# Left-token products of the second weight pair issued ahead of the right half's transposes, and operand sums moved from GpSimd to VectorE

## What is computed

```python
# first block: mixer, then
x = x + gt_m * rms_norm(y_mix @ w_out, g_post_mix)                # "down" 0, e = 0
h = rms_norm(x, g_pre_ffn) * (1 + sc_f) + sh_f                    # boundary 1
gate, val = split(dwconv3(h @ w_up))                              # "up" conv
x = x + gt_f * rms_norm((gelu(gate) * val) @ w_down, g_post_ffn)  # "down" far, e = 1
# second block
# boundary 2
x = layernorm(ALPHA * x + 0.5 * (silu(x @ w1) * (x @ w3)) @ w2)   # "up" 1
x = layernorm(ALPHA * x + mixer(x))                               # "down" mix2, e = 3
# boundary 3
x = layernorm(ALPHA * x + 0.5 * (silu(x @ w1) * (x @ w3)) @ w2)   # "up" 2
```

## Time and profile before

| | us |
|---|---|
| median of three runs (lowest, highest) | 3124.21 (3119.46, 3126.83) |
| span of the profiled execution | 3115.5 |
| PE busy | 2934.1 (94%) |
| DVE busy | 2196.2 (70%) |
| ACT busy | 1251.5 (40%) |
| POOL busy | 282.6 (9%) |

### The profile page before, as it was taken

One profiled execution on the slowest core, in us unless ns is written; L12 is line 12 of the kernel. 1 busy time (PEld: TensorE's weight loads), 2 busy tenths in 40 slices (PEclk: granted clock), 3 DMA queues, 4 the chain that ended last, 5 costly groups with the idle time before them and its releaser, 6 DMA issues.

```text
span 3115.5 us, 36782 instructions
## 1 busy us (share of the span) xinstructions
PE 2934.1 (94%) x13273; PEld 2307.7 (74%) x13273; DVE 2196.2 (70%) x3919; ACT 1251.5 (40%) x2186; POOL 282.6 (9%) x287
## 2 busy tenths in 40 slices
PE   7998889799999999999999998997999799999997
PEld 4875667578888888788888875774547678888886
DVE  7888516989988567766665675999525866665668
ACT  3123435544444554433334443245543333333443
POOL 2141200200000002000000001214420200000000
PEclk9988989899999999999999999998999999999999
DMA  6531023244445773444448632110004344444854
GB/s 226 169 125 21 9 98 119 71 156 156 162 158 195 272 253 109 147 158 159 156 152 316 217 129 66 41 44 16 1 0 152 106 151 156 156 156 167 316 200 148
DMA packets 345410, 436.79 MB, mean 140 GB/s; under 512 B 29685, under 2 KB 191517, under 8 KB 345054
## 3 DMA queue, kind: packets, MB, share of 16 engines
q1 hardware_dynamic: 342274, 428.46, 41.4%
q10 hardware_dynamic: 2956, 5.99, 0.5%
HBM read 317.59 MB, written 116.50 MB: 139 GB/s over the span
## 4 chain that ended last, share of the span: by engine, by line
PE 81%; DVE 12%; ACT 3%; issue 2%; DMA 2%; POOL 1%; SPq 0%; DVEq 0%; ACTq 0%; POOLq 0%
PE psum L1902 35%; PE psum L1359 20%; PE psum L2714 5%; PE psum L1017 5%; PE psum L1893 3%; PE psum L3914 3%; DVE count_junk L3135 2%; PE psum L2904 2%; PE psum L2883 1%; PE psum L414 1%; DMA ada_w<-in_w_ada 1%; PE psum L384 1%; PE psum L3822 1%; DVE x_t L1600 1%; PE psum L2894 1%
## 5 line engine op out<-in xcount | busy, mean ns | idle before, releaser
L1359 PE MATMUL psum<-far_op,far_op 128*128 128x512 f32 x2772 | 629.6, 389 | 0.0
L1359 PEld LDWEIGHTS psum<-far_op,far_op 128*128 128x128 f32 x2772 | 520.0, 188 | 108.2 <-issue 0.3
L1902 PE MATMUL psum<-x_b,w_near 128*128 128x512 f32 x1440 | 347.6, 390 | 3.9 <-DVE w_near L1531 3.9
L1902 PE MATMUL psum<-x_t,w_near 128*128 128x512 f32 x1440 | 337.0, 389 | 0.7 <-ACT psum L1640 0.6
L1902 PE MATMUL psum<-x_t,w_far 128*128 128x512 f32 x1440 | 336.3, 389 | 0.0
L1902 PEld LDWEIGHTS psum<-x_b,w_near 128*128 128x128 f32 x1440 | 271.3, 188 | 60.9 <-issue 4.3
L1902 PEld LDWEIGHTS psum<-x_t,w_near 128*128 128x128 f32 x1440 | 270.0, 188 | 58.0 <-ACT psum L1640 2.0
L1902 PEld LDWEIGHTS psum<-x_t,w_far 128*128 128x128 f32 x1440 | 270.2, 188 | 56.5 <-ACT u_keep L1652 0.4
L1130 DVE TENSOR_TENSOR far_op<-far_a,far_op 128x512 fp32r<-128x512 f32 x231 | 160.7, 695 | 176.2 <-ACT far_op L1123 174.8
L1123 ACT CAST far_op<-far_a 128x512 fp32r<-128x512 f32 x231 | 143.9, 623 | 316.0 <-PE psum L1359 307.9
L1902 PE MATMUL psum<-x_b,w_far 128*128 128x512 f32 x720 | 178.0, 397 | 8.8 <-DVE val_row L1772 8.8
(11 more groups left out here) (499 smaller groups left out, 4967.6 us busy)
## 6 DMA issues: line engine op xcount, KB each, us to landing
far_a<-row_ops SPq DMA_DIRECT2D x231, 256.0 KB, 2.8
row_ops<-hidden SPq DMA_DIRECT2D x99, 512.0 KB, 5.6
raw<-in_ffn_w SPq DMA_DIRECT2D x88, 512.0 KB, 4.5
col_sums<-hidden SPq DMA_DIRECT2D x66, 512.0 KB, 5.7
far_b<-col_sums SPq DMA_DIRECT2D x132, 256.0 KB, 3.2
raw<-in_w_up SPq DMA_DIRECT2D x44, 512.0 KB, 3.8
hidden<-in_ffn_w SPq DMA_DIRECT2D x44, 512.0 KB, 5.1
far_b<-in_ffn_w SPq DMA_DIRECT2D x66, 256.0 KB, 3.2
```

Of the source, the lines that this page charges most:

```text
L1359: ins = t.matmul(bank(b + n), l[slot][:, rows], r[slot][:], start=(fresh and i == 0 and m == 0), stop=(i == FH - 1 and m == 2), skip_group ...
L1902: ins = t.matmul(bank(b), at[:, l, cols], x[:, k, r], start=(start and k == 0 and m == 0), stop=(k == 3 and m == 2), skip_group_check=not ...
```

## The change

At boundaries 1 and 3 (`begun_ahead`) TensorE multiplies, after the left half of pair 0 and before it waits for the right rows, the left half of pair 1: all eight columns of weight 0 and the first four of weight 1 (`ahead`), into banks 4 and 6. The right half's transposes then have banks 5 and 7 only, and two columns are transposed first instead of four. The casts and rests of both of pair 1's first operands are moved ahead of the norm chain of the right rows. `up_tensor` leaves out what was done ahead. The junk tile of the squares moves to another place, since the operand of weight 1 now lies there during the squares.

At all three boundaries `t_pools` goes: VectorE makes the sums b11 ahead of the right columns' rests, b21 in between the first four, and t1 behind the last.

```diff
-    sq_junk = place("sq_junk", [P, 2, HALF], RR + 40 * KB)
+    sq_junk = place("sq_junk", [P, 2, HALF], GR + 84 * KB)
...
-    def t_pools(pool, st):
...
+    def first_sum(dve, st, j):
+        if j == 0:
+            dve.wait_ge(x_lo_made, st.turned(0, 3))
+        nc.vector.tensor_tensor(b11_sum[j][:], x_op["b11"][:, j, 0], x_op["b11"][:, j, 1], ALU.add).then_inc(t_raw, 1)
+
+    def late_sum(dve, st, j):
+        if j == 0:
+            dve.wait_ge(x_lo_made, st.turned(0, KD - 1))
+        nc.vector.tensor_tensor(b21_sum[j][:], x_op["b21"][:, j, 0], x_op["b21"][:, j, 1], ALU.add).then_inc(t_raw, 1)
+
+    def left_differences(dve, st):
         for j in range(4):
+            dve.wait_ge(t_raw, st.first_summed(j))
+            dve.wait_ge(x_kept, st.kept_x(j))
+            nc.vector.tensor_tensor(t_part("t1", j, 1), t_part("t3", j, 0), b11_sum[j][:], ALU.subtract).then_inc(t_raw, 1)
...
     def up_scalar(act, st):
-        cast_op(act, st, 1, 1)
+        if not begun_ahead(st):
+            cast_op(act, st, 1, 1)
         t_upper(act, st, 0)
...
     def up_vector(dve, st):
-        rest_op(dve, st, 1, 1)
+        if not begun_ahead(st):
+            rest_op(dve, st, 1, 1)
+        left_differences(dve, st)
         for wave in range(3):
             t_waves(dve, st, wave)
...
     def up_tensor(pe, st):
                 for half in range(2):
-                    ins = classic_step(1, u, k, half, k == 0, k == KD - 1)
+                    if half or not (begun_ahead(st) and ahead(u, k)):
+                        ins = classic_step(1, u, k, half, k == 0, k == KD - 1)
...
     def end_scalar(act, st, up):
         upper_first(act, up)
+        for i in range(2):
+            cast_op(act, up, 1, i)
         take_root(act, cols_of(1))
...
-        cast_op(act, up, 1, 0)
         upper_second(act, up)
...
     def end_vector(dve, v, steps, st, up):
         lower_first(dve, v, up)
+        for i in range(2):
+            rest_op(dve, up, 1, i)
         if e == 0:
...
+    def begun_ahead(st):
+        return st.e in (0, 3)
+
+    def turn_bank(up, half, k):
+        if half and begun_ahead(up):
+            return bank(5 + 2 * (k % 2))
         return bank(4 + k % 4)
+
+    def ahead(u, k):
+        return u == 0 or k < 4
...
     def lower_second(dve, v, up):
+        for j in range(4):
+            first_sum(dve, up, j)
         for k in range(KD):
...
             v.tensor_tensor(lower, src, upper, ALU.subtract).then_inc(x_lo_made, 1)
-            if k == 3:
+            if k < 4:
+                late_sum(dve, up, k)
+            if k == 3 and not begun_ahead(up):
                 rest_op(dve, up, 1, 0)
...
     def end_tensor_up(pe, st, up):
         def turn(half, k):
-            if half and k < 4:
-                pe.wait_ge(x_lo_made, up.turned(0, k + 4))
+            if half and k < 2:
+                pe.wait_ge(x_lo_made, up.turned(0, KD - 1))
             elif half:
-                pe.wait_ge(x_kept, up.kept_x(k - 4))
+                pe.wait_ge(x_kept, up.kept_x(k - 2))
...
-            for k in range(4):
+            lead = 2 if half else 4
+            for k in range(lead):
                 turn(half, k)
...
-                if k + 4 < KD:
-                    turn(half, k + 4)
+                if k + lead < KD:
+                    turn(half, k + lead)
+            if half == 0:
+                for u in range(2):
+                    pe.wait_ge(op_lo, up.op(1, u))
+                    for k in range(KD):
+                        if ahead(u, k):
+                            classic_step(1, u, k, 0, k == 0, k == KD - 1)
...
     def blocks_gpsimd(pool, steps):
-        t_pools(pool, up_conv)
-        t_pools(pool, up_1)
         mix2_gpsimd(pool, steps)
-        t_pools(pool, up_2)
```

More of the change, by code:

```diff
@@ L780, in body @@
     rows_mm, ROWS_0 = glu_mm, 6
-    t_pool, T_POOL_0 = win_lo, len(win_units)
+    t_raw, T_RAW_0 = win_lo, len(win_units)
     before = {"units": 0, "evac": 0, "ups": 0, "act": 0}
@@ L915, in summed, with first_summed, late_summed, t1_made @@
             return T_SUM_0 + 12 * self.q + 4 * wave + j + 1
-        def pooled(self, i):
-            return T_POOL_0 + 12 * self.q + i + 1
+        def first_summed(self, j):
+            return T_RAW_0 + 12 * self.q + j + 1
+        def late_summed(self, j):
+            return T_RAW_0 + 12 * self.q + 4 + j + 1
+        def t1_made(self, j):
+            return T_RAW_0 + 12 * self.q + 8 + j + 1
         def t_made(self, o, j):
@@ L1547, in t_part @@
         return x_f32[name][:, j, part]
-    def t_pools(pool, st):
-        g = nc.gpsimd
-        pool.wait_ge(x_lo_made, st.turned(0, KD - 1))
-        pool.wait_ge(x_hi_made, st.turned(1, 0))
-        for j in range(4):
[L1555 to L1561, removed]
+    def first_sum(dve, st, j):
[7 more added lines that the diff above has]
+    def left_differences(dve, st):
+        for j in range(4):
+            dve.wait_ge(t_raw, st.first_summed(j))
+            dve.wait_ge(x_kept, st.kept_x(j))
+            nc.vector.tensor_tensor(t_part("t1", j, 1), t_part("t3", j, 0), b11_sum[j][:], ALU.subtract).then_inc(t_raw, 1)
     def t_waves(dve, st, wave):
@@ L1570, in t_waves @@
                 dve.wait_ge(x_kept, st.kept_x(4 + j))
-                dve.wait_ge(t_pool, st.pooled(4 + j))
+                dve.wait_ge(t_raw, st.t1_made(j))
                 ins = v.tensor_tensor(t2, b22, t1, ALU.subtract)
@@ L1576, in t_waves @@
                 dve.wait_ge(t_sum, st.summed(0, j))
-                dve.wait_ge(t_pool, st.pooled(8 + j))
+                dve.wait_ge(t_raw, st.late_summed(j))
                 ins = v.tensor_tensor(t4, b21_sum[j][:], t2, ALU.subtract)
@@ L1587, in t_upper @@
             if o == 2:
-                act.wait_ge(t_pool, st.pooled(4 + j))
+                act.wait_ge(t_raw, st.t1_made(j))
             else:
@@ L2246, in far_end_ln @@
         split_columns(dve, v, 1)
-    def turn_bank(k):
+    def begun_ahead(st):
[3 more added lines that the diff above has]
+            return bank(5 + 2 * (k % 2))
         return bank(4 + k % 4)
+    def ahead(u, k):
+        return u == 0 or k < 4
     def kept_column(k):
@@ L2265, in upper_first @@
                 act.wait_ge(xt_turned, up.turned(0, k))
-                s.copy(upper, turn_bank(k)).then_inc(x_hi_made, 1)
+                s.copy(upper, turn_bank(up, 0, k)).then_inc(x_hi_made, 1)
             if e == 0 and k % 2:
@@ L2277, in rest @@
             dve.wait_ge(x_hi_made, up.turned(0, k))
-            src = split_tmp[k % 2][:] if up.e == 0 else turn_bank(k)
+            src = split_tmp[k % 2][:] if up.e == 0 else turn_bank(up, 0, k)
             v.tensor_tensor(lower, src, upper, ALU.subtract).then_inc(x_lo_made, 1)
@@ L2284, in lower_first @@
                     dve.wait_ge(x_lo_made, up.turned(0, k - 2))
-                v.tensor_scalar(split_tmp[k % 2][:], turn_bank(k), mod_cols[:, 3, k:k + 1], mod_cols[:, 2, k:k + 1],
+                v.tensor_scalar(split_tmp[k % 2][:], turn_bank(up, 0, k), mod_cols[:, 3, k:k + 1], mod_cols[:, 2, k:k + 1],
                                 ALU.mult, ALU.add).then_inc(xt_tmp, 1)
@@ L2300, in keep @@
                 act.wait_ge(xt_turned, up.turned(1, k))
-                s.activation(kept_column(k), turn_bank(k), ACT.Identity, scale=mod_cols[:, 3, k:k + 1],
+                s.activation(kept_column(k), turn_bank(up, 1, k), ACT.Identity, scale=mod_cols[:, 3, k:k + 1],
                              bias=mod_cols[:, 2, k:k + 1]).then_inc(x_kept, 1)
@@ L2304, in keep @@
                 act.wait_ge(x_lo_made, up.turned(1, k))
-                s.copy(kept_column(k), turn_bank(k)).then_inc(x_kept, 1)
+                s.copy(kept_column(k), turn_bank(up, 1, k)).then_inc(x_kept, 1)
         def upper(k):
@@ L2312, in upper @@
                 act.wait_ge(xt_turned, up.turned(1, k))
-                s.copy(x_columns(1, k)[0], turn_bank(k)).then_inc(x_hi_made, 1)
+                s.copy(x_columns(1, k)[0], turn_bank(up, 1, k)).then_inc(x_hi_made, 1)
         if up.e == 0:
@@ L2332, in lower_second @@
             dve.wait_ge(x_hi_made, up.turned(1, k))
-            src = kept_column(k) if up.e == 0 else turn_bank(k)
+            src = kept_column(k) if up.e == 0 else turn_bank(up, 1, k)
             v.tensor_tensor(lower, src, upper, ALU.subtract).then_inc(x_lo_made, 1)
-            if k == 3:
+            if k < 4:
+                late_sum(dve, up, k)
+            if k == 3 and not begun_ahead(up):
                 rest_op(dve, up, 1, 0)
@@ L2385, in far_turn @@
         for n in range(HN):
-            ins = nc.tensor.transpose(turn_bank(k)[:, P * n:P * (n + 1)], res_block(HN * half + n, k), ident[:])
+            ins = nc.tensor.transpose(turn_bank(up, half, k)[:, P * n:P * (n + 1)], res_block(HN * half + n, k), ident[:])
         ins.then_inc(xt_turned, 1)
@@ L2438, in turn @@
                 row = scaled_block(HN * half + n, k) if e == 0 else res_block(HN * half + n, k)
```

(2 more changed lines are left out.)

## The result

The changed kernel took 3142.24 us (median of four runs, 3139.17 to 3144.83) against 3123.12 for the kernel before beside it: ratio 1.007, 95% interval 1.0058 to 1.0082; that is 19 us slower by the medians and 22 by the ratio. The forecast was 3144.3, in the range 3131 to 3150, slower with a chance of 0.85. The span of the profiled execution is 3137.4 us, 21.9 more than before.

A forecast was written before the change was run, and what follows sets the result against it. VectorE, not TensorE, was taken to set the first boundary's end. The three boundaries, 19.6 + 0 + 0.5 = +20.1 us, added to the median of 3124.2 gave 3144.3, range 3131 to 3150.

The forecast's parts named there:

- The norm's delay: Casts and rests ahead of the norm delay its factors by 2.7 us at the first boundary, 2.1 at the third.
- The serialized loop: First boundary, right half: with two banks TensorE, ScalarE and VectorE take turns; 37.5 us instead of 18.0, +19.5 us.
- The clock: First boundary's loop: most steps stay at the low clock, 5.7 us each, against 4.15 at the full clock.
- the rival with all steps at the full clock: First boundary: same serialization but all steps at 2.4 GHz; +12.1 us, 3136, chance 0.20.
- VectorE behind the last column: First boundary: weight rest and t2 differences, 7.4 us, become t1 and t2 differences, 4.8 us; -2.6 us.
- Second boundary: From the far products (e = 1): only the sums move, nothing is gained; 0, within 0.5 us either way.
- Third boundary: At e = 3: loop does not serialize, moved products turn into waits, about 3 us inside pair 1; +0.5 us.
- Two banks suffice: Rival: first boundary's right loop nearly keeps its 1.82 us step; +1.4 us, 3125.6, chance 0.09.
- TensorE's work counts: Rival: VectorE's pair 2 operand is ready when TensorE ends pair 1; -11.6 us, 3112.6, chance 0.06.
- The total: Whole kernel: the three boundaries sum to +20.1 us on a span of 3115.5; forecast 3144.3.

The follow-up runs named there:

- experiment 1: The changed kernel with ScalarE's right-half order at e = 0 made keep(k), upper(k) instead of keep(k + 1) first; 3125.43 us, ratio 1.003.
- experiment 4: The changed kernel with only weight 0 of pair 1 ahead, three banks and a lead of three for the right transposes, old ScalarE order; 3118.3 us, ratio 1.0.
- experiment 3: The changed kernel with the operand sums left on GpSimd, products ahead and two banks kept; 3139.33 us, ratio 1.0071.
- experiment 5: The changed kernel with 36 thrown-away matmuls in TensorE's wait before the first boundary's right half; 3142.95 us, ratio 1.0079.
- keep_then_cast: The same run as experiment 1: the changed kernel with keep(k), upper(k) on ScalarE at e = 0; 3125.43 us, ratio 1.003.
- experiment 2: The changed kernel without products ahead, with old casts, rests, four banks and lead 4; only the sums on VectorE; 3113.11 us, ratio 0.9983.
- warm_start: The same run as experiment 5: the changed kernel with 36 thrown-away matmuls before the first boundary's right half; 3142.95 us, ratio 1.0079.
- sums_only: The same run as experiment 2: the changed kernel without products ahead, only the sums on VectorE; 3113.11 us, ratio 0.9983.

## Why the prediction was right, point by point

- *The norm's delay.* Forecast +2.7. The factors came 10.3 us behind the stretch's first products before and 12.9 after (532.82 to 543.11, 533.76 to 546.63): +2.6. At the third boundary +2.1 was forecast (its terms 0.4, 1.2 and 0.6 add up to 2.2) and 2.1 came.
- *The serialized loop.* Forecast 37.5 us from the first transpose to VectorE's end of the last right column, at steps of 5.7 and one faster; it was 37.8 (564.08 to 601.88) with four steps of 5.7 to 5.9 and two of 4.9 to 5.1. That the sum is this close is partly luck: the low steps were up to 0.2 longer than the 5.7 taken, since six products took 2.73 us there and not 2.5, and in place of one step near 4.15 two ran partly at the low clock. Experiments 1 and 4 show by two different edits that the circle is bank lead plus ScalarE's order, and 3 that it does not need the sums on VectorE.
- *The clock.* Most steps ran low, as taken. Experiment 5 shows that the loop brings the clock down from the full level, so the rival with all steps at the full clock did not come about even from a full-clock start. The Trainium skill's sentence that activity releases the throttle (TensorE: Matmul & The Clock Gate, "What's actually happening") fits keep_then_cast, whose loop rose, and this one, which did not stay up.
- *VectorE behind the last column.* Forecast -2.6: t1 and t2 took 4.82 us (601.88 to 606.70) against 7.39 before. With +0.3 from a weight load for which VectorE waited longer (1.05 us, before 0.74) the first boundary sums to 2.6 + 19.8 - 2.6 + 0.3 = 20.1, forecast 19.6.
- *Second boundary.* Forecast 0, measured -0.4, but as two terms: TensorE now waited 1.24 us for the first right column, because the four b11 sums stand ahead of its rest. I had costed them at nothing here, as at e = 0, where they did fit ahead of the first rest. The left products, 1.6 us faster by the clock, hid it; that the sum came out at nearly 0 is luck.
- *Third boundary.* Forecast +0.5, measured +0.9. The last column came 16.8 us behind the first transposes (forecast 16.4), since the first products took 2.7 us at the low clock and not 2.2; VectorE's list behind it took 21.3 us (2502.62 to 2523.93), forecast 20.8. The 2.83 us wait inside pair 1 was forecast at about 3.
- *The rivals.* "Two banks suffice" failed at e = 0 and held at e = 3, and at e = 0 once ScalarE's order was changed. The Trainium skill's rule on rotating banks that stood beside it (Perfetto Trace Analysis, "Matmuls") is borne out at e = 3 by 1.83 us a step; at e = 0 the measurement is against it, 5.9 us a step with the same two banks, until ScalarE's order was changed. "TensorE's work counts" failed at VectorE's list: from the last column to pair 2's operand it took 24.7 us (601.96 to 626.61), as forecast. Experiment 2 shows the other side of it: work taken off that list comes back as time.
- *The total.* Forecast +20.1; the spans differ by 21.9, the medians by 19.1.

What stays open: about 1.3 us of the 21.9 us of span lie outside the three stretches, 0.9 of them ahead of the first one, where nothing was edited. B3 moves by 1.7 us among three kernels with the same program there (the changed one, keep_then_cast, warm_start), so its +0.9 alone would not be evidence.

## What to carry to other kernels

Before a rotation of buffers is shortened, write down for one element which instruction of each engine stands ahead of the one that frees or fills it; a copy of element k + 1 placed ahead of the cast of element k needs one buffer more; here four banks gave steps of 1.8 us, three 2.1 and two 5.9. Filling an engine's gap moves the end only if that engine ends the stretch; here the 8.2 us came back as waits, while in sums_only VectorE had t2 some 5 us earlier with GpSimd out of its way, and that was worth 4.7. Work put into a gap must take its preparations (here two casts and rests) from another pause, not from the head of the chain that the gap waits for; at the last boundary that was 2.1 us.

## What I had not expected of the hardware

The loop with its 2.10 us pauses let the clock switch to and fro: stretches of 6 us show 0.50, 0.78, 0.51 and 0.77 in turn, and in warm_start, where the clock was 1.00 until 564, the first products behind a 2.33 us pause took 2.93 us. Pauses of 0.42 us in every second step (keep_then_cast) left products at 1.63 to 1.66 us for six, the full clock.
